# Delta-rule layer: pool products and part of the out-projection placed between other steps, pair products in two bank pairs

## What is computed

```
X   = kk St + Aak V                (64 x 64 per head)
y   = r St + (T Arb)' X + Ark V
St' = decay * (St + (T B)' X + K V)
```

## Time and profile before

| | |
|---|---|
| median of three runs | 1509.59 us |
| profiled execution: its own time | 1508.68 us |
| its span | 1506.9 us |
| PE busy (share) | 1276.4 us (85%) |
| DVE / ACT / POOL busy | 450.9 / 274.4 / 270.6 us |
| DMA | 496.4 MB, mean 329 GB/s |
| stages 2 to 6 of the even layer, on PE | 443.54 to 513.31 us of the span |

### The profile page before, as it was taken

How to read it: one execution, slowest core, us unless ns; L and a number is a source line. 1 busy time by engine, 2 the same in 40 slices (tenths; PEclk the granted TensorE clock), 3 DMA queues, 4 the chain that set the end, 5 groups by cost and what they waited for, 6 DMA issues and landing times. The chain is left out here.

```text
span 1506.9 us, 21513 instructions
## 1 busy us (share of the span) xinstructions
PE 1276.4 (85%) x9120; PEld 689.4 (46%) x9120; DVE 450.9 (30%) x893; ACT 274.4 (18%) x543; POOL 270.6 (18%) x163
## 2 busy tenths in 40 slices
PE   9999999999998999767667667999998776676577
PEld 5755466546877544223223323856544322232232
DVE  2554653645746521101000101295411010010011
ACT  2142400323422222100000000115211110011010
POOL 0676226742022009920000000000000000000000
PEclk9999999999999999888888999999999888899889
DMA  9932363236631899999999999946899999999997
GB/s 371 366 136 84 145 246 112 112 112 260 261 141 38 337 388 408 431 432 432 434 431 432 431 432 423 395 169 244 338 435 428 432 431 431 431 432 431 432 433 315
DMA packets 34066, 496.40 MB, mean 329 GB/s; under 512 B 5456, under 2 KB 8400, under 8 KB 11728
## 3 DMA queue, kind: packets, MB, share of 16 engines
q1 hardware_dynamic: 34000, 495.45, 79.1%
HBM read 493.34 MB, written 2.10 MB: 329 GB/s over the span
## 5 line engine op out<-in xcount | busy, mean ns | idle before, releaser
L3341 PE MATMUL banks<-weight_ring,spare_weights_arena 128*32 128x512 f32 x1472 | 207.3, 713 | 131.2 <-DMA weight_ring<-in_moe_weights 129.3
L3233 DVE TENSOR_TENSOR spare_weights_arena<-spare_weights_arena,banks 64x512 f32<-64x512 f32 x32 | 22.1, 691 | 652.9 <-ACT spare_weights_arena L3142 652.9
L3341 PEld LDWEIGHTS banks<-weight_ring,spare_weights_arena 128*32 128x32 f32 x1472 | 53.0, 127 | 277.1 <-issue 212.1
L3285 PE MATMUL banks<-spare_weights_arena,x 128*128 128x64 f32 x960 | 110.5, 273 | 0.0
L3285 PEld LDWEIGHTS banks<-spare_weights_arena,x 128*128 128x128 f32 x960 | 109.6, 192 | 0.0
L3142 ACT ACTIVATE spare_weights_arena<-banks 64x512 f32<-64x512 f32 x32 | 18.9, 591 | 484.1 <-PE banks L3341 484.1
L3359 PE MATMUL banks<-weight_ring,spare_weights_arena 128*32 128x512 f32 x688 | 87.8, 654 | 12.3 <-issue 7.6
L1005 POOL TENSOR_TENSOR weight_ring<-spare_weights_arena,weight_ring 128x2048 f32<-128x2048 f32 x16 | 74.0, 4636 | 70.8 <-DVE spare_weights_arena L849 38.5
L1118 PE MATMUL banks<-weight_ring,x_normed_hT_mix 128*128 128x512 f32 x192 | 84.7, 592 | 0.0
L3411 PE MATMUL banks<-spare_weights_arena 64*128 64x512 f32 x240 | 59.6, 614 | 20.9 <-ACT spare_weights_arena L3150 20.9
L3341 PE MATMUL banks<-x_normed_hT_mix,spare_weights_arena 128*32 128x512 f32 x272 | 41.4, 759 | 31.4 <-DMA x_normed_hT_mix<-in_moe_weights 31.4
(11 more groups left out here) (557 smaller groups left out, 1796.3 us busy)
## 6 DMA issues: line engine op xcount, KB each, us to landing
weight_ring<-in_moe_weights SPq DMA_DIRECT2D x52, 4096.0 KB, 25.1
weight_ring<-in_ring_weights SPq DMA_DIRECT2D x35, 2048.0 KB, 12.3
weight_ring<-in_moe_weights SPq DMA_DIRECT2D x28, 2048.0 KB, 11.9
spare_weights_arena<-in_moe_weights SPq DMA_DIRECT2D x13, 4096.0 KB, 54.0
x_normed_hT_mix<-in_moe_weights SPq DMA_DIRECT2D x6, 4096.0 KB, 52.1
spare_weights_arena<-in_moe_weights SPq DMA_DIRECT2D x8, 2048.0 KB, 12.3
weight_ring<-in_moe_weights SPq DMA_DIRECT2D x10, 1024.0 KB, 6.6
x_normed_hT_mix<-in_moe_weights SPq DMA_DIRECT2D x8, 1024.0 KB, 7.0
```

Of the source, the lines that this page charges most:

```text
L3233: dve.tensor_tensor(hid[0:2 * CAP, :], sil[0:2 * CAP, :], b_gu[2 * CAP:4 * CAP, :], ALU.mult).then_inc(s_h, 1)
L3285: ins = pe.matmul((b_x, b_dn)[k // 4][:, k % 4 * 2 * CAP:(k % 4 + 1) * 2 * CAP], g.x[:, tt, k * P:(k + 1) * P], Pr[:, tt, :], start=(tt == ...
L3341: ins = pe.matmul(b_gu[q:q + CAP, :], xg[:, 2 * quarter + k, e * CAP:(e + 1) * CAP], up_w(where, quarter, k)[:, which, e, :], start=(quart ...
```

## The change

What it does:

- **Pool products.** `pool_diff(q)` and `pool_out(q)`, one of the four groups each, are called by `beside(lev, step)` between the steps of levels 1 and 2 of the inverse, in banks 6 and 7. ACT's copies are placed behind its copies of the levels.
- **Out-projection.** Six k tiles of results 0 and 1 (`out_part(0, (4,))` to `out_part(1, (5,))`) stand behind steps 1 and 3 of levels 3 to 5, the last two behind chunks 0 and 1 of the recurrence. The banks of the four results are now 6, 7, 0, 1.
- **`Aak V` and `Ark V`.** Before the inverse only chunk 0's `Aak V` is left. `Aak V` of a later chunk is added up in PSUM with `kk St`. `Ark V` and key times value become one product with a stationary operand of 128 columns, `[Ark | K]` (`of_kr`); `[B | Arb]` is laid out likewise (`of_br`).
- **The recurrence.** For chunk c a pair of banks `PAIR[c] + q` (2, 3 or 4, 5) takes, for the heads of parity q, y in one half of the partitions and the new state in the other: the value product, `r St`, the state itself through an identity product, and `GH'X` with all 128 columns of `GH` as the stationary operand. Heads go by parity (all four of q = 0, then all four of q = 1). ACT copies X's even heads and y, DVE X's odd heads, and DVE makes the state with one multiplication per parity.
- **Bonus and gate.** The eight operations on `c1` and `gn` move from DVE to POOL, behind the inverse.
- **Waits.** SP waits for `s_dS` 8 where it waited for `s_y` 2.

The core of the diff:

```
+        def beside(lev, step):
+            if lev == 1:
+                pool_diff(step)
+            elif lev == 2:
+                pool_out(step)
+            elif step % 2:
+                n = 2 * (lev - 3) + step // 2
+                pe.wait_ge(s_pyc, 4)
+                out_part(n // 4, (4 + n % 4,))
...
-        for out, left in ((4, Aak), (6, Ark)):
-            for tt in range(TT):
-                for h in range(8):
-                    for c2 in range(2):
-                        hs = slice(h * 64, (h + 1) * 64)
-                        ins = pe.matmul(ps[out + tt][rows[c2], hs], left[rows[c2], h % 2, tt, h // 2, :],
-                                        vn[rows[c2], tt, hs], start=(out == 4 or h == 0), stop=(out == 4))
...
+        def of_values(c):
+            t, tt = rows[c % 2], c // 2
+            for h in range(8):
+                ins = pe.matmul(ps[PAIR[c] + h % 2][:, of_head(h)], both(of_kr[t, tt], h), vn[t, tt, hs[h]],
+                                start=(h < 2), stop=False, skip_group_check=True)
+            ins.then_inc(s_V, 1)
+        for h in range(8):
+            ins = pe.matmul(ps[4][rows[0], hs[h]], Aak[rows[0], h % 2, 0, h // 2, :], vn[rows[0], 0, hs[h]], start=True, stop=True)
+        ins.then_inc(s_AV, 1)
...
                     turn(tt, ps[4 + tt])
+                beside(lev, tt)
             for tt in range(TT):
                 T_step(lev, tt)
+                beside(lev, 2 + tt)
...
+            if c:
+                pe.wait_ge(s_XV, c)
+                for q in range(2):
+                    pe.wait_ge(s_S, 2 * (c - 1) + q + 1)
+                    for n in range(4):
+                        ins = pe.matmul(x_at(c, 2 * n + q), kk[rows[q], n, tk], St[c % 2][rows[q], n, :], start=False, stop=(n == 3),
+                                        skip_group_check=True)
+                    ins.then_inc(s_X, 1)
+                pe.wait_ge(s_V, c + 1)
+                for q in range(2):
+                    for n in range(4):
+                        ins = pe.matmul(ps[PAIR[c] + q][rows[1 - q], of_head(2 * n)], r[rows[q], n, tk], St[c % 2][rows[q], n, :],
+                                        start=False, stop=False, skip_group_check=True)
+                    if c < 3:
+                        ins = pe.matmul(ps[PAIR[c] + q][rows[q], 0:256], ident[rows[q], rows[q]],
+                                        St[c % 2][rows[q]].rearrange("p a i -> p (a i)"), start=False, stop=False,
+                                        skip_group_check=True)
+                ins.then_inc(s_rS, 1)
+                pe.wait_ge(s_rS, c)
+            for q in range(2):
+                if c:
+                    pe.wait_ge((s_Xc, s_Xd)[q], c)
+                for n in range(4):
+                    ins = pe.matmul(ps[PAIR[c] + q][:, of_head(2 * n)], GH[t, q, tt, n, :],
+                                    x_of(c, 2 * n + q), start=False, stop=(n == 3), skip_group_check=True)
+                ins.then_inc(s_dS, 1)
+            if c == 0:
                 pe.wait_ge(s_GHc, TT)
                 pe.wait_ge(s_up, 10)
+            if c < 2:
+                out_part(1, (6 + c,))
+            if c < 3:
+                next_t = rows[(c + 1) % 2]
                 for h in range(8):
+                    ins = pe.matmul(x_at(c + 1, h), Aak[next_t, h % 2, (c + 1) // 2, h // 2, :],
+                                    vn[next_t, (c + 1) // 2, hs[h]], start=(h < 2), stop=False, skip_group_check=True)
+                ins.then_inc(s_XV, 1)
+                if c:
+                    pe.wait_ge(s_ye, 2 * c)
+                of_values(c + 1)
...
-        out_part(0, (4, 5, 6, 7))
-        out_part(1, (4, 5, 6, 7))
         out_part(2, (4, 5, 6, 7))
+        out_part(3, (4, 5, 6, 7)).then_inc(s_w, 1)
         mix_transposes(0)
-        out_part(3, (4, 5, 6, 7)).then_inc(s_w, 1)
         pe.wait_ge(s_mT, 1)
```

More of the change, by code:

```diff
@@ L1399, in even_layer @@
     blocks = lambda ap: ap.rearrange("p (q a i t) -> p q a i t", q=2, a=TT, i=4)
-    Aab, Aak, Ark = blocks(flat(L)), blocks(flat(E)), blocks(q1)
-    AB = xs_flat.rearrange("p (q a i n) -> p q a i n", q=2, a=TT, i=4)
+    Aab, Aak = blocks(flat(L)), blocks(flat(E))
+    four = lambda ap: ap.rearrange("p (a i x t) -> p a i x t", a=TT, i=4, x=4)
+    of_kr, of_br = four(a_q1), four(xs_flat)
+    both = lambda ap, h: ap[:, h // 2, 2 * (h % 2):2 * (h % 2) + 2, :].rearrange("p x t -> p (x t)")
     GH = flat(m[:, 4:12, :]).rearrange("p (q a i n) -> p q a i n", q=2, a=TT, i=4)
@@ L1587, in _, with pool_diff_copy, pool_scaled @@
             act.copy(of_tile(T_flat, tt), ps[2 + tt]).then_inc(s_T0c, 1)
-        act.wait_ge(s_sh, 7)
-        for q in range(2):
-            act.wait_ge(s_pd, q + 1)
-            act.copy(dT[:, 2 * q:2 * q + 2, :], bank2(ps[q])).then_inc(s_pdc, 1)
-        for tt in range(TT):
[L1593 to L1598, removed]
+        act.wait_ge(s_AV, 1)
+        act.copy(AkV, ps[4][0:64, :]).then_inc(s_AVc, 1)
+        def pool_diff_copy(q):
+            act.wait_ge(s_pd, q + 1)
+            act.copy(dT[:, 2 * q:2 * q + 2, :], bank2(ps[6 + q])).then_inc(s_pdc, 1)
+        def pool_scaled(q):
+            act.wait_ge(s_py, q // 2 + 1)
+            act.activation(g.mixT[:, 4 + q, :], ps[6 + q // 2][:, (q % 2) * S:(q % 2 + 1) * S], ACT.Copy,
+                           scale=pscale[:, q:q + 1]).then_inc(s_pyc, 1)
+        act.wait_ge(s_sh, 7)
         for lev in range(1, 6):
@@ L1744, in normed @@
             m8, v8, r8 = (c[:, 8 * tt:8 * tt + 8] for c in (mu_, var, rstd))
[L1745 to L1756, removed]
+            dve.wait_ge(s_ye, (4, 7)[tt])
+            if tt == 1:
+                dve.wait_ge(s_yr, 1)
             link(dve, dve.tensor_reduce(m8, h8(yt), AX.X, ALU.add))
@@ L1915, in _, with pool_out, out_part @@
                 ins.then_inc(s_pd, 1)
+        def pool_out(q):
+            pe.wait_ge(s_par, 48)
+            pe.wait_ge(s_pdc, 2)
+            ins = pe.matmul(ps[6 + q // 2][:, (q % 2) * S:(q % 2 + 1) * S], pool_w[:, q, :], dT[:, q, :],
+                            start=True, stop=True)
+            if q % 2:
+                ins.then_inc(s_py, 1)
+        def out_part(j, ks):
+            tt, ch = divmod(j, 2)
+            w = g.chunk(pe, c0 + (5 if ks[0] >= 4 else 6))
+            for kt in ks:
+                ins = pe.matmul(ps[OUT_BANK[j]], g.mixT[:, kt, tt * P:(tt + 1) * P], w[:, 4 * ch + kt % 4, :],
+                                start=(kt == 4), stop=(kt == 3))
+            return ins
+        def beside(lev, step):
+            if lev == 1:
+                pool_diff(step)
+            elif lev == 2:
+                pool_out(step)
[3 more added lines that the diff above has]
+                out_part(n // 4, (4 + n % 4,))
         def turn(tt, bank):
@@ L1950, in off_times_T @@
                 pe.wait_ge(s_Tu, 2 * (lev - 2) + tt + 1)
-            elif tt == 1:
-                pe.wait_ge(s_pyc, 4)
             for q, n in heads:
@@ L1986, in _ @@
                         ins = pe.matmul(ps[4 * (1 - tt) + q][rows[c2], i * P:(i + 1) * P], T[rows[c2], q, tt, i, :],
[L1987 removed]
+                                        both(of_br[rows[c2], tt], 2 * i + q), start=True, stop=True)
                 ins.then_inc(s_GH, 1)
         pe.wait_ge(s_up, 9)
[L1991 to L2001 removed]
+        of_values(0)
+        x_of = lambda c, h: (X[rows[c % 2], hs[h]] if c else AkV[:, hs[h]])
+        x_at = lambda c, h: ps[h % 2][rows[c % 2], of_head(h)]
         pe.wait_ge(s_GHc, 1)
@@ L2020, in _ @@
-                ins.then_inc(s_rS, 1)
-                pe.wait_ge(s_Xc, 2 * c)
-            if c < 3:
-                for h in range(8):
-                    ins = pe.matmul(state_at(c, h), GH[t, h % 2, tt, h // 2, 64:128], x_of(c, h), start=False, stop=(h >= 6))
-                ins.then_inc(s_dS, 1)
-            for h in range(8):
-                ins = pe.matmul(ps[6 + tt][t, hs[h]], GH[t, h % 2, tt, h // 2, 0:64], x_of(c, h), start=False, stop=(h == 7))
-                if c < 2:
-                    of_values(c + 1, h)
```

163 lines of the change are left out of this document (70 added, 93 removed).

## The result

The changed kernel takes 1533.57 us (median of four runs, 1527.3 to 1541.06) where the kernel before takes 1509.45 in the same comparison: ratio 1.0162 [1.0109, 1.0214] (in brackets, here and below, the 95% interval). It is slower, as forecast, but by 24 us and not 14, and outside the range (1515.5 to 1527.5). It also varies by 14 us from run to run, where before varied by 2.3. The profiled execution took 1529.83 us, its span is 1528.0: 21.1 us longer than before.

What follows compares the result with a forecast made beforehand. PE was taken to bound the even layer from 443.54 to 513.31 us. Terms -8.0 + 10.1 + 18.3 - 6.2 = +14.2 on 1508.68 gave 1522.9, by the median 1523.8; it said 1523.5, range 1515.5 to 1527.5.

Steps and rivals of the forecast that it cites:

- The failed step: Whole even layer: granted clock stays at 1.00 (2.4 GHz) because PE is not made idler; no term for it.
- `kk St`, `r St`, the identity: Recurrence: 96 products by parity at 0.068 us, 6.5; identity products 8 x 0.222, 1.8; possible overlap up to 0.9, not taken.
- the self-wait: Recurrence: PE waits for its own `r St` products before `GH'X`, 3 x 0.25 = 0.75 us.
- a change of form: Recurrence: some 14 switches between product forms at 0.1 us, 1.4; inverse: nine stand-alone pieces at 0.13, 1.2.
- The wait in level 3: Inverse, level 3, step 1: PE stands 0.8 us for the fourth scaled pool copy.
- The uncovered copy: Out-projection: `out_part(3, pool)` no longer covers the wait for the copy of `mix_transposes(0)`, +0.75 us.
- Norms were hidden as argued: Out-projection: both norms finish before PE asks for them, with 2 us to spare.
- Loads hidden: Rival, 128-column products: weight loads overlap running products, 0.068 us each, +8.8 in all, so 1518; chance 0.2.
- More serial: Rival: form changes and PE's self-waits cost 0.3 us each, or second norm late; +3 to +5 more, 1528; chance 0.1.
- Concurrency kept: Rival, recurrence: all new products overlap at 0.032 us, sum -1.6, 1508; decides below 0.038 a product; chance 0.04.
- The delay swallowed: Rival: something other than the even layer sets the start of the experts' stream, time stays near 1510; chance 0.06.
- One for one: End of the even layer moves the start of the experts' weight stream, and the program's end, by the same amount.

Runs made afterwards that it cites:

- The sparse and the full block: Kernel before plus, between recurrence and out-projection, 256 instructions of the 64-row, 128-column form (sparse): 1565.98 us; or 64 full products (full): 1538.16 us.
- the many full products: Changed kernel plus four idle 128x128 products of 256 moving columns behind each value product and four behind each `r St`: 1533.94 us, ratio 1.0158.
- the first experiment: Changed kernel with value products and `GH'X` each cut into two 64-column halves, writing the two partition halves in turn: 1510.8 us, ratio 1.0005.

## Why the prediction fell short

**The failed step.** "PE is not made idler, so I change nothing there" was the sentence on the clock. Its premise held, PE is idle for 0.17 of 33.87 us in the recurrence, and its conclusion did not. The clock went to 1.2 GHz for 24 us of the profiled run, 11 to 12 us that stand in no term. Without them the profiled time would have been 1518 to 1519, inside the range. The spread goes with the missing term: over the four runs the share of the clock not granted, (1 - mean clock) times the span, is 102.4 us at a span of 1528.0, 113.9 at 1539.3, 99.2 at 1525.5 and 109.0 at 1535.5. From the shortest to the longest it grows by 14.7 and the span by 13.8. The sparse and the full block show cause and effect on the kernel before. In the changed kernel it is shown by the halves, with which the clock holds, and by the many full products, with which it all but holds.

**The sum without it.** At full clock the stages measured (forecast behind each): up to the inverse 445.16 - 443.54 = 1.6 (1.4); inverse 29.6 (31.0); GH 3.6 (3.3); recurrence 33.87 less half of 494.2 to 512.27, 24.8, or 25.8 piece by piece (29.5); out-projection 21.99 less half of 512.27 to 518.1, 19.1 (18.8). Together 78.8 to 79.8, that is +9 to +10 over 69.77, against +14.2. Work alone would have given 1517.8 to 1518.8: the sum was 4 to 5 us too high, and by luck this hid part of the miss.
- *Prices.* 0.110 for the two 128-column forms was near, if low: 0.114 to 0.120, so that 128 of them took some 15.2 us and not 14.1. 0.068 for one quarter measured 0.067. The estimate by the Trainium skill (TensorE: Matmul & The Clock Gate, section LDWEIGHTS; 13.7 us for the same 128) was 1.5 us low.
- *Mis-sized: `kk St`, `r St`, the identity.* 32 x 0.068 + 4 x 0.222 with the self-wait and a change of form is 3.4 us a chunk. Chunk 1 shows 488.02 - 486.16 = 1.86. Where I allowed at most 0.9 us for all three chunks in the bounds, it is 1.5 in each of chunks 1 and 2 and some 1.0 in the last, 4 us together: the second parity's products run while the first's and the identity products do, in other quarters, as the interleaved rows at 487.03 show. That is most of what the recurrence came out lower (3.7 to 4.7).
- *Inverse.* The wait in level 3 was 0.49 and not 0.8, and the changes of form cost less than 9 x 0.13.
- *Out-projection.* The uncovered copy measured 0.67 us for 0.75. Norms were hidden as argued, and not only because the slow clock stretched their cover: in the first experiment, at 1.00, PE waits for none either.

**The rivals.** Loads hidden: refuted, 0.117. More serial: its 1528 came near the profiled time by chance, its mechanism didn't occur, since the work was less serial than summed. Concurrency kept: false for the products as written. The halves stand 0.034 us apart, but two of them make one product of the rival, which wanted less than 0.038 for the whole; that the 1510.8 they give is near its 1508 is chance. For a pair of halves the price is 0.068, the one that "Loads hidden" put down. The delay swallowed: refuted, 20.95 us at the experts' start and 21.1 at the end. "One for one" and "PE's work is the bound" held.

**What stays open.** Which property of the work the clock goes by was not separated: the sparse form differs from the full one in rows, in moving columns, in the time between its products' starts and in its data. In the changed kernel the data are the kernel's own and the clock falls too, so the identity operand is not needed for a fall; whether it hastens one is not shown. Nor is it shown where the longer runs lost more, as one execution of each kernel was profiled. And why the fall came 16 us into the changed recurrence but within 2 us of the inserted block is open: other forms stand between in the first.

## What to carry to other kernels

Where the contraction is 64 rows and the moving columns are 64, in float32, two products on two column halves in turn cost 0.068 us together, one product over both halves costs 0.114 to 0.120: joining small products into one wider instruction can be the dearer way, so read both pitches from the trace first. A busy PE is not a safe clock: when a change replaces dense products by long runs of sparse ones, put a term for half speed and a wider range into the sum, and look at the granted clock of the stretch before anything else. Filling idle time on the engine that bounds is worth at most that idle time, here 4 us, and it came to nothing measurable.

## What the hardware showed that was not expected

- PE busy throughout by the profile and yet at 1.2 GHz: 51 us at 0.50 with the 64-row, 128-column form, 27.57 us at 1.00 with full products in the same place. The Trainium skill (TensorE: Matmul & The Clock Gate, section HAM oscillation — how this bites in real kernels) describes falls that follow from matmul groups separated by waits; the traces here show one without any wait.
- Idle work can be free: 12.4 us of full products left the median where it was (1533.94 against 1533.57, with the latter's runs 14 us apart), with the clock at 0.96 instead of 0.73.
- 64x64x64 products that read the same 64 rows and write the two halves in turn stand 0.034 us apart, those in one quarter 0.067. The Trainium skill (the same page, section The mechanism) lets a weight load overlap a running product only where the row groups differ; here they are the same, and by the pitch something of the two overlaps all the same.
